# Value blocks, attention groups and the first decays of a hybrid decoder layer: the order in which they take turns

## The reference

```python
proj = h @ w_in[l]
aq, ak, av, gq, gk, gv, gr, glr, ga, gb = jnp.split(proj, offsets, axis=-1)
...
scores = where(valid, q @ k.T * DH ** -0.5 + bias, NEG_INF)         # per head
m = maximum(max(scores), sink); p = exp(scores - m)
probs = p / (sum(p) + exp(sink - m)); y_attn = probs @ v
...
gk_log = log_sigmoid(glr @ w_gk_up[l] + b_gk[l]) / 16               # z = glr @ w_gk_up
g = cumsum(gk_log)                                                  # in chunks of 64
q_dec = q * exp(g); k_inv = k * exp(-g); k_to_end = k * exp(g_last - g)
...
merged = sigmoid(ga) * (y_attn @ w_branch_attn) + sigmoid(gb) * (y_gla @ w_branch_gla)
```

## Time and profile before

| what | value |
|---|---|
| median of 3 runs | 1686.44 us (1682.76, 1686.44, 1691.81) |
| the profiled execution's own time | 1683.97 us |
| its span in the trace | 1681.8 us |
| mean granted clock of TensorE | 0.972 of full |
| busy share of the span | PE 96%, PEld 83%, DVE 71%, ACT 49%, POOL 2% |
| chain that ended last, share of the span | PE 91%, DVE 3%, ACT 2%, DMA 2% |

### The profile page before, as it was taken

The page is one execution under the profiler, slowest core; times in us unless marked ns, Lnnn a source line. Parts: engine busy times, 40 slices in busy tenths (PEclk is TensorE's granted clock), DMA queues, the critical chain, the costliest instruction groups (busy, mean ns, idle before and its releaser), DMA issues.

```text
span 1681.8 us, 24152 instructions
## 1 busy us (share of the span) xinstructions
PE 1614.8 (96%) x8963; PEld 1400.2 (83%) x8963; DVE 1194.7 (71%) x1312; ACT 818.5 (49%) x971; POOL 30.4 (2%) x36
## 2 busy tenths in 40 slices
PE   4898889999999999999999799999999999999998
PEld 4777889998789988888888688888888888888887
DVE  5777735658877877988886667666666766789553
ACT  5344435346756653443444455555555555433332
POOL 0000000000002200000000000000000000000000
PEclk8888999999989999999999899999999999999999
DMA  7988877766756789998997366666666666799663
GB/s 284 346 294 304 296 178 258 265 233 200 260 166 213 226 281 341 354 342 323 335 329 255 101 189 190 186 194 188 188 188 190 191 190 188 279 376 348 203 206 114
DMA packets 195235, 411.72 MB, mean 245 GB/s; under 512 B 14754, under 2 KB 19406, under 8 KB 194654
## 3 DMA queue, kind: packets, MB, share of 16 engines
q1 hardware_dynamic: 195006, 410.53, 73.9%
q10 hardware_dynamic: 160, 0.26, 0.0%
HBM read 405.23 MB, written 5.25 MB: 244 GB/s over the span
## 4 chain that ended last, share of the span: by engine, by line
PE 91%; DVE 3%; ACT 2%; DMA 2%; issue 1%; SPq 0%; ACTq 0%; DVEq 0%
PE ps L1358 90%; DMA early<-in_w_ada 1%; DVE colacc L960 1%; DMA stage<-in_w_in 1%; ACT w_hi L601 1%; PE ps L1472 0%; PE ps L1583 0%; PE ps L1725 0%; ACT xnT L622 0%; DVE w_lo L907 0%; PE ps L1679 0%; DVE xr L1269 0%; DVE acc L918 0%; DVE xn L1259 0%; ACT p L772 0%
## 5 line engine op out<-in xcount | busy, mean ns | idle before, releaser
L601 ACT ACTIVATE w_hi<-stage 128x1024 fp32r<-128x1024 f32 x528 | 557.1, 1059 | 740.6 <-PE ps L1358 711.2
L907 DVE TENSOR_TENSOR w_lo<-stage,w_hi 128x1024 fp32r<-128x1024 f32 x528 | 648.9, 1231 | 378.0 <-ACT w_hi L601 376.1
L1358 PE MATMUL ps<-h,w_hi 128*128 128x512 f32 x1408 | 489.4, 394 | 0.0
L1358 PE MATMUL ps<-h,w_lo 128*128 128x256 f32 x1408 | 390.5, 277 | 0.0
L1358 PEld LDWEIGHTS ps<-h,w_hi 128*128 128x128 f32 x1408 | 264.7, 188 | 61.4
L1358 PEld LDWEIGHTS ps<-h,w_lo 128*128 128x128 f32 x1408 | 264.9, 188 | 0.0
L1358 PE MATMUL ps<-h_hi,w_hi 128*128 128x256 f32 x672 | 194.9, 290 | 0.0
L1358 PE MATMUL ps<-h_lo,w_hi 128*128 128x256 f32 x672 | 191.7, 285 | 0.0
L1358 PE MATMUL ps<-h_hi,w_lo 128*128 128x256 f32 x672 | 191.6, 285 | 0.0
L1358 PE MATMUL ps<-w_hi,h_hi 128*128 128x512 f32 (+1 forms) x416 | 170.1, 409 | 4.0 <-DVE w_lo L907 4.0
L1358 PE MATMUL ps<-w_hi,h_lo 128*128 128x512 f32 (+1 forms) x416 | 164.6, 396 | 0.0
(11 more groups left out here) (245 smaller groups left out, 1813.1 us busy)
## 6 DMA issues: line engine op xcount, KB each, us to landing
stage<-in_w_in SPq DMA_DIRECT2D x184, 512.0 KB, 4.0
stage<-in_w_ffn_up SPq DMA_DIRECT2D x176, 512.0 KB, 3.7
ada<-in_w_ada SPq DMA_DIRECT2D x96, 512.0 KB, 6.2
stage<-in_w_ffn_down SPq DMA_DIRECT2D x88, 512.0 KB, 4.8
early<-in_w_ada SPq DMA_DIRECT2D x64, 512.0 KB, 8.5
ada<-in_w_in SPq DMA_DIRECT2D x32, 512.0 KB, 4.8
stage<-in_w_branch_gla SPq DMA_DIRECT2D x32, 512.0 KB, 6.2
stage<-in_w_out SPq DMA_DIRECT2D x32, 512.0 KB, 5.8
```

Of the source, the lines that this page charges most:

```text
L601: act.activation(w_hi[:, u.slot(k)], stage[:, u.slot(k)], ACT.Copy).then_inc(hi_done, 1)
L907: TT(w_lo[:, u.slot(k)], stage[:, u.slot(k)], w_hi[:, u.slot(k)].bitcast(F32), ALU.subtract).then_inc(lo_done, 1)
L1358: return pe.matmul(out, lhsT, rhs, start=start, stop=stop, skip_group_check=True)
```

## The change

- The loops over the query blocks (TensorE, ScalarE, VectorE) and over the gate blocks (TensorE) are written out.
- The z matmuls and ScalarE's copies of them move from value block 0 behind unit 4 of query block 2. `reduce_mod(0)` stays behind unit 0 of value block 0.
- Attention moves one block ahead: `scores(0)` behind unit 4 of query block 3, `scores(g + 1)` in value block g; `probs_back(g)` and `attend(g)` behind units 1 and 2 of value block g.
- In value block 3 the place of a softmax is taken by GLA's `exponents(0)`, `decays(0)`, `cross_decays(0)` and `decayed(0)`. `reduce_mod(1)` moves behind unit 0 of gate block 0.
- The merge's unit 4 is split into `w_hi` and `w_lo` before the last `yg_hi` and `yg_lo`, inside gate block 3.
- `clear_acc` goes; the first `times_c` of the query blocks writes `acc` instead of adding to it. Each softmax on ScalarE now has one `hi` between its two halves in all four groups (before in three).

```diff
 # ScalarE
-            with act.Fori(0, 2) as i:
-                for b in range(2):
-                    u = Run(U_GQK + 8 * b, i, 16)
-                    for k in range(AHEAD, 8 + AHEAD):
-                        hi(u, k)
+            for n in range(4):
+                u = Run(U_GQK + 8 * n)
+                for k in range(AHEAD, 9):
+                    hi(u, k)
+                if n == 2:
+                    for m in range(8):
...
+                        act.activation(lg[:, m], zp, ACT.Identity, bias=V_BGK[:, m:m + 1]).then_inc(z_sb, 1)
+                    act.wait_ge(z_sb, 8)
+                if n == 3:
+                    exps(0, (u, 9))
+                else:
+                    hi(u, 9)
+                hi(u, 10)
+                hi(u, 11)
 # ScalarE, value block g
+                hi(u, 5)
+                probs_out(g)
...
                 hi(u, 6)
-                if g:
-                    attended_hi(g - 1)
+                attended_hi(g)
                 hi(u, 7)
                 hi(u, 8)
                 if g < 3:
+                    exps(g + 1, (u, 9))
+                else:
+                    act.wait_ge(lg_ready, 4)
+                    act.wait_ge(scored, 4)
+                    decays(0)
                     hi(u, 9)
+                    cross_decays(0)
 # VectorE, query block n
+                for k in range(AHEAD, 8):
                     lo(u, k)
+                    times_c(a, k - 4, 4 * n + k - 4, first=n == 0 and k == AHEAD, by=mod)
+                if n == 3:
+                    soft_scores(0)
+                lo(u, 8)
+                lo(u, 9)
+                if n == 3:
+                    soft_probs(0)
 # VectorE, value block g
                 lo(u, 6)
+                attended_lo(g)
                 times_c(a, 2, 4 * g + 2, by=mod)
                 lo(u, 7)
+                if g < 3:
+                    soft_scores(g + 1)
+                else:
+                    dve.wait_ge(lg_ready, 4)
+                    dve.wait_ge(scored, 4)
+                    exponents(0)
+                lo(u, 8)
+                times_c(a, 3, 4 * g + 3, by=mod)
+                lo(u, 9)
+                if g < 3:
+                    soft_probs(g + 1)
+                else:
+                    decayed(0)
 # VectorE and ScalarE, gate block 3 (ScalarE with hi)
+                if n == GH - 1:
+                    lo(Run(U_MERGE), AHEAD)
 # TensorE
+            for n in range(4):
...
+                    unit(u, k, par, h_hi, h_lo, k == 7)
+                    if n == 2 and k == 4:
...
+                            mm(zp, wgk_s[:, m * P:(m + 1) * P], glrT[:], True, True).then_inc(z_ps, 1)
+                    if n == 3 and k == 4:
+                        pe.wait_ge(k_swapped, 32)
+                        pe.wait_ge(z_sb, 8)
+                        scores(0)
 # TensorE, value block g
                     if g == 0 and k == 0:
+                        pe.wait_ge(m_ready, 1)
                         reduce_mod(0)
+                    if k == 1:
+                        probs_back(g)
+                    if k == 2:
+                        attend(g)
+                    if k == 4 and g < 3:
+                        pe.wait_ge(ya_ready, g + 1)
+                        pe.wait_ge(mod_ready, 1)
+                        scores(g + 1)
-            probs_back(3)
-            reduce_mod(1)
-            attend(3)
 # TensorE, gate block n
                 for k in range(2):
                     unit(u, k, par, h_hi, h_lo, False)
+                    if n == 0 and k == 0:
+                        reduce_mod(1)
```

More of the change, by code:

```diff
@@ L741, in attended_hi, with exps @@
                                b7.rearrange("p (n t q) -> p t n q", n=2, t=2), ACT.Copy).then_inc(yahi_done, 1)
[L744 to L747, removed]
+            def exps(g, between):
+                act.wait_ge(m_ready, g + 1)
+                for t in range(NT):
+                    own(act.activation(p0[:, t], p0[:, t], ACT.Exp, bias=nmx[:, 0, t:t + 1], accum_out=rsum[:, 0, t:t + 1]))
+                hi(*between)
+                for t in range(NT):
+                    own(act.activation(p1[:, t], p1[:, t], ACT.Exp, bias=nmx[:, 1, t:t + 1], accum_out=rsum[:, 1, t:t + 1]))
+                act.activation(esk[:], esk[:], ACT.Exp).then_inc(exped, 1)
+            for n in range(4):
[3 more added lines that the diff above has]
+                if n == 2:
                     for m in range(8):
@@ L753, in _ @@
                     act.wait_ge(z_sb, 8)
+                if n == 3:
[4 more added lines that the diff above has]
+                hi(u, 11)
+            for g in range(4):
+                u = Run(U_GV + 8 * g)
+                hi(u, 4)
                 hi(u, 5)
+                probs_out(g)
                 if g:
-                    probs_out(g - 1)
                     act.wait_ge(lg_ready, g)
@@ L822, in _ @@
                 first = U_MERGE + i * MERGE_UNITS
-                for k in range(AHEAD, 8 + AHEAD):
+                for k in range(AHEAD + (i == 0), 8 + AHEAD):
                     hi(Run(first), k)
@@ L1047, in _ @@
             dve.wait_ge(ga_saved, 16 * 4)
[L1048 to L1058, removed]
             def exponents(h):
@@ L1086, in attended_lo, with soft_scores @@
                    ya_hi[:, 2 * g:2 * g + 2].rearrange("p t (n q) -> p t n q", n=2).bitcast(F32), ALU.subtract).then_inc(ya_ready, 1)
[L1089 to L1107, removed]
+            def soft_scores(g):
                 dve.wait_ge(scored, g + 1)
@@ new lines, in _ @@
+            for g in range(4):
+                u = Run(U_GV + 8 * g)
+                a = Run(KT + 4 * g)
+                par = (1 + g) % 2
+                lo(u, 4)
+                if g == 0:
+                    take_ga_col(0)
+                times_c(a, 0, 4 * g, first=g == 0, by=mod)
+                lo(u, 5)
+                times_c(a, 1, 4 * g + 1, by=mod)
+                dve.wait_ge(lnp_ready, g + 1)
+                dve.wait_ge(keep_ready, 1)
+                own(STT(out=lg[:, 2 * g:2 * g + 2], in0=lg[:, 2 * g:2 * g + 2], scalar=0.0, in1=lnp[:], op0=ALU.min, op1=ALU.subtract))
+                own(dve.tensor_tensor_scan(lg[:, 2 * g], keep[:], lg[:, 2 * g], 0.0, ALU.mult, ALU.add))
+                dve.tensor_tensor_scan(lg[:, 2 * g + 1], keep[:], lg[:, 2 * g + 1], 0.0, ALU.mult, ALU.add).then_inc(lg_ready, 1)
+                lo(u, 6)
+                attended_lo(g)
+                times_c(a, 2, 4 * g + 2, by=mod)
+                lo(u, 7)
+                if g < 3:
[11 more added lines that the diff above has]
+                    decayed(0)
+                lo(u, 10)
+                lo(u, 11)
@@ L1190, in _ @@
                 for k in range(AHEAD, 8 + AHEAD):
-                    lo(Run(first), k)
+                    if i or k > AHEAD:
+                        lo(Run(first), k)
                     times_c(a, k - 4, k - 4, first=k == 4)
@@ L1553, in _ @@
             head_sums(2)
[L1556 to L1561, removed]
             def scores(g):
@@ L1634, in _ @@
[L1634 to L1655, removed]
-                    pe.wait_ge(at_ready, i * 4 + (2 * b + 2))
-                    pe.wait_ge(gvh_ready, n + 1)
-                    for j in range(NT):
-                        cols = slice(j * P, (j + 1) * P)
-                        mm(b56[:, j], gvh[:, 0, cols], at[:, 0:T], j % 2 == 0)
-                        f = mm(b56[:, j, P:T], gvh[:, 1, cols], at[:, T:T + P], False, True)
-                    f.then_inc(o_ps, 1)
-                    for k in range(5, 7):
-                        unit(u, k, par, h_hi, h_lo, False)
-                    pe.wait_ge(osq_sum, n + 1)
-                    pe.wait_ge(mod_ready, 2)
-                    mm(hi_b4, ones[:], osq[:, 0], True, True).then_inc(oss_ps, 1)
-                    unit(u, 7, par, h_hi, h_lo, True)
@@ new lines, in _ @@
+                    if k == 1:
[6 more added lines that the diff above has]
+                        scores(g + 1)
+            for n in range(GH):
+                par = (1 + n) % 2
+                u = Run(U_GR + 8 * n)
+                free(par, 5 + (n + 1) // 2)
+                for k in range(2):
+                    unit(u, k, par, h_hi, h_lo, False)
+                    if n == 0 and k == 0:
+                        reduce_mod(1)
+                pe.wait_ge(ya_ready, 4)
+                pe.wait_ge(gla_ready, n + 1)
+                lo64, hi64 = slice(0, CH), slice(CH, P)
+                for rows, c0, w, keys, k0, queries, q0 in (
+                        (lo64, 0, CH, ki, 0, qd, 0), (lo64, CH, CH, kx, 0, qd, CH), (lo64, 2 * CH, 2 * CH, kx, 0, qx, 0),
+                        (lo64, T, CH, ki, 2 * CH, qd, 2 * CH), (lo64, T + CH, CH, kx, 2 * CH, qd, 3 * CH),
+                        (hi64, CH, CH, ki, CH, qd, CH), (hi64, 2 * CH, CH, kx, CH, qd, 2 * CH), (hi64, 3 * CH, CH, kx, CH, qx, 2 * CH),
+                        (hi64, T + CH, CH, ki, 3 * CH, qd, 3 * CH)):
+                    for q in range(2):
```

(17 more changed lines are left out.)

71 lines of the change are left out of this document (26 added, 45 removed).

## The result

The changed kernel takes 1675.84 us (median of 20 runs, 1671.12 to 1685.0), the kernel before 1688.2 (20 runs, 1679.09 to 1696.7). The ratio is 0.9935, 95% interval [0.9914, 0.9956]: faster by 0.65%, about 11 us. The forecast was 1675.6, a gain of 9.6 us.

The account below looks back on a forecast made before the run. TensorE, with 91% of the chain of waits, was taken to bound the kernel. The terms 8.0 + 1.7 - 0.1 gave 9.6 us off 1685.2, so 1675.6 us, range 1670 to 1682.

Parts of the forecast that it names:

- Value block 3 to gate block 0, 8.0 us: TensorE's gap between these blocks, 12.95 us, shrinks to 4.92: gain 8.0, of which 3.6 wait and 4.4 clock.
- The aside on `decayed(0)`: Next possible lateness at the border: covered by some 3 units of value block 3 and two of gate block 0, over 10 us.
- Attention one block ahead, 0: Query block 3 and value blocks: moving attention costs 0, as group 0's 12.9 us is covered by 16.3 us of TensorE work.
- z, 1.7 us: z matmuls moved to query block 2: some 3.7 us instead of 6.94, less 1.5 for a short low clock; gain 1.7.
- the middle of three cases: Clock behind z in query block 2: full gives +3.2 us, low for 6.8 us gives +0.2, short low gives +1.7, taken.
- The loops, 0: Query and gate loops written out: no stall at the query loop's second turn, so gain 0.
- The merge's unit 4, -0.1: Unit 4's early `w_lo` ahead of `yg_hi` and `yg_lo` delays `diag`, for which TensorE waits: 0.1 us lost.
- The sum, 9.6: Whole kernel: 8.0 at the border plus 1.7 for z minus 0.1 in the merge, 9.6 us gained.
- The time, 1675.6: Whole kernel: forecast time 1675.6 us, the gain of 9.6 taken from 1685.2.
- The full clock at z: Rival, query block 2: only a wait lowers the clock, so it stays full; gain 11.1, time 1674.1 us; chance 0.28.
- The clock lost at the border: Rival, gate block 0: the wait goes but the clock still falls; gain 5.2, time 1680.0 us; chance 0.16.
- VectorE as the bound: Rival, value blocks: from 2.9 us more VectorE work or waiting per block, TensorE starves; 8.4 slower, 1693.6 us; chance 0.03.

Follow-up runs that it names:

- run 4: Kernel before with 16 matmuls nobody reads filling TensorE's wait ahead of `probs_back(3)`; ratio to the kernel before 0.9986, first query matmul to merge diag matmul 338.55 us.
- run 9: Changed kernel with GLA's first decays back behind value block 3, attention left one block ahead; no ratio, first query matmul to merge diag matmul 337.12 us.
- run 2: Kernel before with loops written out and only z and its copies moved to query block 2; ratio to the kernel before 1.0017.
- run 6: Changed kernel with z and its copies in two halves, behind units 3 and 4 of query block 2; ratio to the kernel before 0.995.
- run 1: Kernel before with the query and gate loops written out and nothing else moved; ratio to the kernel before 1.0011.
- run 8: Changed kernel with the merge's unit 4 prepared behind `yg_hi` and `yg_lo`, as in the kernel before; ratio to the kernel before 0.9924.
- run 5: The changed kernel again, unaltered, on the chip of the three runs that followed; ratio to the kernel before 0.9941.
- run 10: Changed kernel with two more 128x1024 VectorE copies at the end of value blocks 0 to 2; no ratio, value stage 110.21 us against 108.62.
- run 3: Changed kernel with z back behind the reduction in value block 0; ratio to the kernel before 0.9978.

## Why the prediction was right

- **Value block 3 to gate block 0, 8.0 us: right in size and in its two halves.** The gap is gone, the pieces are as long as at full clock (transposes 1.22, `attend` 1.93, reduction 1.71 us), and run 4 shows the clock's share as 4.2 us where 4.4 was said. The aside on `decayed(0)` was right that it is covered, but gave too much: it starts at 473.48 and TensorE's first small matmul of GLA comes at 483.13, so the cover is 9.6 us and not more than 10, and under one unit of its own block is left by then, not three. VectorE is done with `qx` at 476.26. Run 9 shows that the early place is needed.
- **Attention one block ahead, 0: right.** The cover of group 0 was given as 16.3 us against 12.9. In the profile, VectorE's part ends at 369.70 + 1.22 = 370.92 and the transposes start at 374.21, 3.3 us to spare where 3.4 was said:

```profile
358.26 0.42 DVE L1090 SCALAR_TENSOR_TENSOR p<-ps,bias 128x256 f32<-128x256 f32 x1 [0.91 <-PE ps L1381]
...
369.70 1.22 DVE L1105 TENSOR_TENSOR p<-p,rsum 128x1024 f32<-128x1024 f32 x1
```

- **z, 1.7 us: 1.4 in run 2 over the two stages that it touches.** The low stretch is 3.4 us long, as in the row it was priced from. The trace before gave no mechanism for its length; the middle of three cases was picked, so that it came out is in part luck. z takes 3.98, not 3.7, and two errors in its working partly cancelled: the last two tiles start at 330.79, 2.9 us behind the first and not 3.1, and take 1.06, not 0.6. Six tiles fill nearly all of those 2.9 us by themselves, so that the copies were waited for only 0.2 us (run 6). The rule in the Trainium skill (TensorE: Matmul & The Clock Gate, What's actually happening), that idleness lowers the clock, would have had it at 1.00 here. The trace disagrees: 30.23 of 30.30 us busy ahead of the fall at 332.3. Matmuls with 16 rows of weights did not hold the clock up, and in two groups with a weight unit between they did no harm.

```profile
302.00:332.30 30.30, 30.23 (x236) 29.00 (x235) 20.14 (x17) 13.42 (x17) 0.00 (x0) 1.00 0.76 247
```

- **The loops, 0: right** (run 1). What the Trainium skill (Runtime: NRT & Kernel Launch, Instruction fetch mechanics) says of taken branches, a stall where the target lies outside the part already fetched, cost nothing that shows in these loops.
- **The merge's unit 4, -0.1: it is -0.2** (run 8). Ahead of `yg_lo` VectorE idles for 0.19 where it idles for 1.13 in run 8, but one more `w_lo` stands there, 1.14 from start to start, so `yg_lo` starts 0.2 later and TensorE's wait for diag grows from 1.5 to 1.7. VectorE after:

```profile
597.30 1.23 DVE L916 TENSOR_TENSOR w_lo<-stage,w_hi 128x1024 fp32r<-128x1024 f32 x1 [0.19 <-ACT w_hi L601]
598.44 1.22 DVE L1195 TENSOR_TENSOR yg_lo<-yt,yg_hi 128x1024 fp32r<-128x1024 f32 x1
```

- **The sum, 9.6, against 9.06 in the stretch.** 0.3 of the difference is z, 0.1 the merge, and some 0.1 I did not trace. The span shrank by 10.4, 0.8 of it ahead of the first query matmul and 0.5 behind diag. Neither can be put down to the change: the same kernel's stretch starts 1.5 us later in run 5, and the 0.5 lies in the up-projection, where the instructions are the same.
- **The time, 1675.6 against 1675.84: luck to this closeness.** The forecast started from 1685.2, and the kernel before has a median of 1688.2 over 20 runs. The medians differ by 12.4 us, the stretch by 9.06. What the forecast had right is the stretch.
- **The rivals.** The full clock at z did not come. The clock lost at the border did not come, though run 9 shows it is near. VectorE as the bound did not come either, but the point from which it decides was put too far off: not 2.9 us more per block but less than 1.4, and at `ya_lo` (run 10).

## What to carry to other kernels

Price a wait of the bounding engine with what the clock does behind it: here 3.6 us of waiting cost 8.0, and filling the wait with matmuls nobody reads gave more than half of that back. Put small matmuls (few rows, one column) in short groups between dense units: the reduction of 1.7 us and z in halves of 1.9 us did not lower the clock, z in one piece of 4 us did. And measure a slack at each handover that can be late, since an engine's free time in the block as a whole (2.9 us here, against 0.9 at `ya_lo`) says too little. The start of a list counts as much as its length: in run 9 the length was right, and the 2.5 us before it were missing.

## What was not expected

The up-projection, far behind the change, runs at one of two rates, and which one differs between executions of the same program. Two executions of the changed kernel, the first and run 5, at 1000 to 1100 us:

```profile
1000.00:1100.00 100.00, 100.00 (x579) 87.47 (x578) 69.66 (x84) 55.99 (x66) 0.00 (x0) 1.00 0.65 189
```

```profile
1000.00:1100.00 100.00, 100.00 (x569) 86.73 (x567) 66.98 (x78) 54.00 (x62) 0.00 (x0) 1.00 0.64 184
```

579 matmuls against 569 in 100 us, no wait of TensorE and clock 1.00 in both. The one span is 1671.4 us, the other 1682.3. Of the 14 profiled executions of this study, eight had the higher rate and six the lower, the kernel before and the changed one among the higher. From its first matmul to the first of the down-projection, the up-projection takes 488.7 to 489.5 us in the eight and 498.1 to 499.2 in the six. Between the two executions above it makes 9.3 of the 10.9 us; 1.5 more lie ahead of the stretch. The other runs have no trace, but differences of this size fit their spread, and they are why ratios here don't tell 3 us apart. What sets the rate is open; nothing was tried on it.

Second, the low clock came three times without any wait of TensorE: behind reduction and z before, behind z after, and for 10.2 us in run 3.
